# Two attention blocks on one core: a loop written out, head steps moved by one point, weights loaded in two halves

## What is computed

```python
# block 1: 32 query heads of 64 in 4 groups, window 128, per-head bias and sink
q, k, v, gate = split(rms(x) @ swa_w_in)
q, k = rms_norm(q, q_gain), rms_norm(k, k_gain)
p = exp(s - m); p = p / (sum(p) + exp(sink - m))
x = x + ((p @ v) * silu(gate)) @ swa_w_out
# block 2: 8 heads of differential attention (df) and 8 of stick-breaking attention (sb)
proj = rms(concat(meta, x)) @ w_in      # sb q,k,v,g and df q,k,v,g, each 1024 wide
dq = partial_rope(rms_norm_2(dq, q_norm_w)); dk = partial_rope(rms_norm_2(dk, k_norm_w))
df_o = (softmax(s0) - lam * softmax(s1)) @ dv        # then rms norm over 128
sb_o = exp(log_beta + tail) @ sb_v                   # tail: reversed cumulated log_keep
out = x + concat(sb_o * silu(sb_g), df_o * silu(df_g)) @ w_out
```

## Time and profile before

| | us |
|---|---|
| median of 3 runs (2010.58 to 2016.63) | 2014.16 |
| the profiled execution, its own time | 2015.65 |
| its span, first to last instruction | 2014.0 |
| PE busy | 1928.9 (96%) |
| PE weight loads busy | 1547.7 (77%) |
| DVE busy | 921.3 (46%) |
| ACT busy | 828.4 (41%) |
| POOL busy | 36.2 (2%) |

### The profile page before, as it was taken

The page is one execution under the profiler, slowest core; times in us unless marked ns, Lnnn a source line. Parts: engine busy times, 40 slices in busy tenths (PEclk is TensorE's granted clock), DMA queues, the critical chain, the costliest instruction groups (busy, mean ns, idle before and its releaser), DMA issues.

```text
span 2014.0 us, 28665 instructions
## 1 busy us (share of the span) xinstructions
PE 1928.9 (96%) x9868; PEld 1547.7 (77%) x9868; DVE 921.3 (46%) x2325; ACT 828.4 (41%) x1831; POOL 36.2 (2%) x65
## 2 busy tenths in 40 slices
PE   4999999898998999999999999999999999988999
PEld 3777777676776888878788887888878888766887
DVE  4355555555556333544445444454444445444222
ACT  5355455454555332534335343343433435244221
POOL 1000000000000000000000000000000000000000
PEclk9999999999998999999999999999999999989999
DMA  6932223122224445322222222222222322204553
GB/s 149 203 89 70 72 74 87 55 82 60 81 55 115 126 140 148 86 66 83 65 68 80 64 64 66 81 67 77 65 66 65 83 62 64 64 21 121 132 144 83
DMA packets 298414, 173.34 MB, mean 86 GB/s; under 512 B 23040, under 2 KB 289824, under 8 KB 297824
## 3 DMA queue, kind: packets, MB, share of 16 engines
q1 hardware_dynamic: 292976, 157.55, 29.1%
q0 software_dynamic: 4352, 13.98, 2.6%
q10 hardware_dynamic: 1024, 1.07, 0.3%
HBM read 156.86 MB, written 14.66 MB: 85 GB/s over the span
## 4 chain that ended last, share of the span: by engine, by line
PE 73%; ACT 9%; DVE 7%; issue 7%; DMA 3%; ACTq 1%; DVEq 0%; SPq 0%
PE G L448 58%; PE S L710 2%; ACT wh L853 2%; ACT p L940 2%; PE G L547 2%; DMA raw<-in_swa_w_in 1%; PE O L727 1%; PE S L755 1%; PE O L783 1%; ACTq L1113 1%; ACT pT L949 1%; ACT st L942 1%; PE T L701 1%; PE G L672 1%; DVE st L1352 1%
## 5 line engine op out<-in xcount | busy, mean ns | idle before, releaser
L448 PE MATMUL G<-xh,wh 128*128 128x512 f32 (+1 forms) x2624 | 898.0, 374 | 7.8 <-DVE xl L1424 4.8
L448 PE MATMUL G<-xl,wh 128*128 128x512 f32 (+1 forms) x2624 | 845.8, 354 | 0.0
L448 PE MATMUL G<-xh,wl 128*128 128x512 f32 (+1 forms) x2624 | 842.7, 353 | 0.0
L1270 DVE TENSOR_TENSOR wl<-raw,wh 128x512 fp32r<-128x512 f32 x528 | 353.8, 688 | 550.8 <-ACT wh L853 539.1
L448 PEld LDWEIGHTS G<-xh,wh 128*128 128x128 f32 x2624 | 465.8, 190 | 107.8 <-issue 36.0
L448 PEld LDWEIGHTS G<-xh,wl 128*128 128x128 f32 x2624 | 462.9, 189 | 70.1
L448 PEld LDWEIGHTS G<-xl,wh 128*128 128x128 f32 x2624 | 463.1, 189 | 66.0 <-issue 6.9
L853 ACT ACTIVATE wh<-raw 128x512 fp32r<-128x512 f32 x528 | 313.0, 619 | 190.8 <-DMA raw<-in_w_out 97.4
L1147 ACT ACTIVATE att<-att,st 128x144 f32<-128x144 f32 (+3 forms) x64 | 36.9, 576 | 187.9 <-DVE wmeta L1609 103.3
L940 ACT ACTIVATE p<-p,st 128x256 f32<-128x256 f32 (+1 forms) x128 | 60.8, 475 | 124.6 <-DVE st L1339 124.6
L1339 DVE CUSTOM_DVE_ANT_0 p<-S,bias,sink_u 128x256 f32<-128x256 f32 (+1 forms) x128 | 56.1, 442 | 0.0
(11 more groups left out here) (216 smaller groups left out, 1699.2 us busy)
## 6 DMA issues: line engine op xcount, KB each, us to landing
raw<-in_w_in SPq DMA_DIRECT2D x56, 1024.0 KB, 6.0
raw<-in_swa_w_in SPq DMA_DIRECT2D x32, 1024.0 KB, 5.5
raw<-in_swa_w_out SPq DMA_DIRECT2D x16, 1024.0 KB, 6.2
raw<-in_w_out SPq DMA_DIRECT2D x16, 1024.0 KB, 6.4
raw<-in_w_in POOLq DMA_DIRECT2D x8, 1024.0 KB, 7.4
rel_rows<-relb SPq DMA_DIRECT2D x1, 6128.0 KB, 36.7
mixed<-in_x SPq DMA_DIRECT2D x4, 1024.0 KB, 10.0
raw<-in_swa_w_in SPq DMA_DIRECT2D x8, 512.0 KB, 7.2
```

What stands on the lines that cost most here:

```text
L448: mm = pe.matmul(d, w[:, slot, k, :], v[:, k, a:b], start=(k == 0 and n == 0), stop=(k == KC - 1 and n == 2))
L1270: V.tensor_tensor(wl[:, slot, q, :], raw[:, slot, q, :], wh[:, slot, q, :].bitcast(F32), ALU.subtract).then_inc(w_lo, 1)
```

## The change

1. The loop over i = 1 to 3 of the first block is written out on all five engines. The instructions are the same ones in the same order, with constants in place of registers.
2. Each 1 MB weight load of SP becomes two of 512 KB. The first half is issued when DVE has split two quarters of the tile that held the slot, the second half when it has split all four. ACT waits for the first half before quarter 0 and for the second (`raw_late`) before quarter 2. The eight loads of sbq on POOL and those of the key and value tiles stay whole.
3. In `finish`, for dfq and dfk, the statistic on PE moves from point 1 to 2, the reciprocal root on ACT from 2 to 3, the scaling on DVE from 3 to 4, the four transfers on ACT from 4 to 5, and the three rotary passes on DVE from 6 to 7. OWNERS2 and its waits stay as they are.

```diff
-        gate_in, sbq_in = sem("gate_in"), sem("sbq_in")
+        raw_late = [sem(f"raw_late{i}") for i in range(2)]
+        sbq_in = sem("sbq_in")
@@ SP: weights()
-                after(sp, w_lo, 4 * (tile - 2) + 4)
-                sp.dma_start(raw[:, slot, :, :], w_v[:, :, ds(col, P)]).then_inc(raw_in[slot], 16)
+                for part, s in enumerate((raw_in[slot], raw_late[slot])):
+                    c = slice(part * KC // 2, part * KC // 2 + KC // 2)
+                    after(sp, w_lo, 4 * (tile - 2) + 2 * part + 2)
+                    sp.dma_start(raw[:, slot, c, :], w_v[:, c, ds(col, P)]).then_inc(s, 16)
@@ SP, POOL, PE, ACT, DVE alike
-            with sp.Fori(1, UNITS) as i:
+            for i in range(1, UNITS):
@@ ACT: split()
+                if quarter == 2 and loaded[0] is raw_in[slot] and len(loaded) == 2:
+                    act.wait_ge(raw_late[slot], loaded[1] - KV_LOADS)
@@ PE: finish()
-                    if p == 1:
+                    if p == 2:
                         norm_stat(two, 2 * h + ti + 1)
@@ ACT: finish()
-                    if p == 2:
+                    if p == 3:
                         after(act, n_stat, count)
...
-                    if p == 4:
+                    if p == 5:
                         buf, width = (dfk, ALL) if ti else (dfq, TOK)
@@ DVE: finish()
-                    if p == 3:
+                    if p == 4:
                         after(dve, n_rs, count)
...
-                    if p == 6:
+                    if p == 7:
                         after(dve, n_rot, 64 * count)
```

More of the change, by code:

```diff
@@ L310, in unit_loads @@
                 weights(T_UNIT + 2 * u, 0, w1_v, P * (4 * g + i))
-                after(sp, w_lo, 4 * (T_UNIT + 2 * u - 1) + 4)
-                sp.dma_start(raw[:, 1, :, :], w1_v[:, :, ds(SWA_GATE + P * (4 * g + i), P)]).then_inc(gate_in, 16)
+                weights(T_UNIT + 2 * u + 1, 1, w1_v, SWA_GATE + P * (4 * g + i))
             for g in range(KV):
                 unit_loads(0, g)
-            with sp.Fori(1, UNITS) as i:
+            for i in range(1, UNITS):
                 for g in range(KV):
@@ L418, in _ @@
                 sinks_of(0, g)
-            with pool.Fori(1, UNITS) as i:
+            for i in range(1, UNITS):
                 for g in range(KV):
@@ L581, in _ @@
                 swa_window(0, g, attend=g > 0)
-            with pe.Fori(1, UNITS) as i:
+            for i in range(1, UNITS):
                 for g in range(KV):
@@ L825, in _ @@
             KV_LOADS = 2 * 16 * (KV // 2)
-            OUT1_LOADS = (KV_LOADS + 16 * 4 * UNITS, KV_LOADS)
+            OUT1_LOADS = (KV_LOADS + 16 * 4 * UNITS, KV_LOADS + 16 * 4 * UNITS)
             HEAD_LOADS = tuple(n + 16 * (KC // 2) for n in OUT1_LOADS)
@@ L830, in kv_loaded @@
             def kv_loaded(g):
-                return (raw_in[g % 2], 32 * (g // 2 + 1)) if g < KV else unit_loaded(0, 0)
+                return (raw_in[g % 2], 32 * (g // 2 + 1), "whole") if g < KV else unit_loaded(0, 0)
             def unit_loaded(u, half):
-                return (gate_in, 16 * (u + 1)) if half else (raw_in[0], KV_LOADS + 16 * (u + 1))
+                return raw_in[half], KV_LOADS + 16 * (u + 1)
             def out_loaded(loads, i, slot):
@@ L846, in split @@
             def split(pair, slot, quarter, loaded):
+                if quarter == 2 and loaded[0] is raw_in[slot] and len(loaded) == 2:
+                    act.wait_ge(raw_late[slot], loaded[1] - KV_LOADS)
                 if quarter == 0:
-                    act.wait_ge(*loaded)
+                    act.wait_ge(*loaded[0:2])
                     after(act, tile_done, 2 * pair + slot - 1)
@@ L998, in _ @@
                 swa_window(0, g, attend=g > 0)
-            with act.Fori(1, UNITS) as i:
+            for i in range(1, UNITS):
                 for g in range(KV):
@@ L1414, in _ @@
                 swa_window(0, g, attend=g > 0)
-            with dve.Fori(1, UNITS) as i:
+            for i in range(1, UNITS):
                 for g in range(KV):
```

## The result

The changed kernel takes 2029.14 us (median of 5 runs, 2025.29 to 2032.61) against 2014.16 us before. The ratio is 1.0075 with a 95% interval of 1.0055 to 1.0096, so it is slower by 15 us. The forecast was 2019.1 us with a range of 2009 to 2029: the sign was right, the loss three times too small, and the time lies just outside the range. What came out is nearly rival B's 2030 us. Of the experiments' runs one is left out of its figure: an execution of e1_unroll that took 2820 us at a mean granted clock of 0.626.

A forecast was written before the change was run, and what follows sets the result against it. PE's own instruction stream was taken to bound heads 1 to 7, with under 0.2 us margin at tile boundaries. -11.6 - 1.5 + 17.5 + 0.5 = +4.9 us on 2014.16 gave 2019.1 us, range 2009 to 2029.

The forecast's parts named there:

- rival B: Heads: new stops also slow PE's clock, each head losing 1.5 us more; +10.7 us in sum, 2030 us; chance 0.08.
- Part 1: First block: writing out the loop saves 11.6 us, covering both jumps back and register costs per unit.
- Part 2: First query tile: the first half load lands sooner, cutting PE's wait for the squares; -1.5 us.
- Part 3: Heads: later statistic and rotary steps make PE wait; +17.5 us over seven heads, +0.5 in head 0.
- A head costs 2.4 - 1.0 + 1.0 = 2.4 to 2.5 us: Each of heads 1 to 7: dfq wait, less the returned statistic stop, plus dfk wait.
- The wait for dfq: Start of tile dfv: PE waits 2.4 us for dfq's last rotary pass, ending at 1209.05 against 1206.64 wanted.
- The walk through the three engines: One head, followed through PE, ACT and DVE: 12.7 us from dfq's statistic to its last rotary pass.
- The wait for dfk: Start of tile dfg: PE waits 1.0 us more for dfk's last rotary pass.
- The credit for the statistic's stop: Dfk's statistic finds its squares ready; the 0.83 us stop and queue refilling return about 1.0 us a head.
- The granted clock: Heads: clock loss behind new stops, left out of the forecast sum; as a rival 1.5 us a head, chance 0.08.
- A: Heads: PE doesn't wait at the banks and the statistic's stop goes; -20.1 us, 1994 us; chance 0.17.
- C: First block: writing out brings nothing, instruction stalls come at intervals of code; +6.4, 2020.6 us with half loads; chance 0.05.

The follow-up runs named there:

- e1_unroll: Kernel before with only the first block's loop written out on all five engines: 2002.20 us, ratio 0.9940.
- e6: Kernel before with the first block's loop written out on VectorE (DVE) alone, loops kept on the other four engines: 2007.04 us, ratio 0.9959.
- e11: Kernel before, loop kept, with the query tile's weight load in units 4 to 15 issued one quarter of VectorE's splits later: 2010.44 us, ratio 0.9969.
- e2: Kernel before with only the weight loads in two halves, loop and steps as before: 2008.93 us, ratio 0.9975.
- e8: Changed kernel with only the three rotary passes put back to point 6; statistic, root, scaling and transfers stay one point later: 2004.27 us, ratio 0.9951.
- e3: Kernel before with only the statistic and rotary steps one point later: 2046.04 us, ratio 1.0149.
- e10: Kernel before with only the banks of dfq and dfk released by n_ln, the statistic's last reader: 2013.45 us, ratio 0.9990.
- e7: Changed kernel with statistic, root, scaling and transfers at their old points, only the three rotary passes one point later: 2027.11 us, ratio 1.0060.
- e5: Changed kernel with dfv, dfg and sbq waiting for n_ln (last reader of the banks) instead of the last rotary pass: 1985.97 us, ratio 0.9857.

## Why the prediction was right or wrong

**Part 1, the loop written out: right.** Forecast -11.6. The units took 10.9 us less between the first two points shown (32.1 us each), and e1 alone is 12 us faster. What the forecast took from the Trainium skill (Runtime: NRT & Kernel Launch, Instruction fetch mechanics), that a taken branch out of the two pages in memory must fetch before it goes on, is borne out by e6, where the two stops go with VectorE's loop, and by the row of instructions in e11. The stop was 5.1 us with 1 MB of weights under way, 3.3 with 0.5 MB, and 2.6 with none. That half loads would also shorten it I had missed. It made no difference to the sum, since the change removes the jumps themselves.

**Part 2, the half loads: right in size.** Forecast -1.5 at the first query tile. The changed kernel is 1.96 us ahead there, and TensorE's wait for the squares fell from 2.76 to 0.49 us. It was forecast at about 1.2. The half was there 1.2 us behind the end of the write of `rel_rows` (91.08 and 89.89), and not 1.4. In e2, with the same loads, that write ended 1.3 us later than before, the wait is 1.38 us and the kernel 0.8 us ahead, so the size differs from one profile to the next.

**Part 3, the steps: the mechanism right, the sum too small by half.** The step that failed is the sum of a head, "A head costs 2.4 - 1.0 + 1.0 = 2.4 to 2.5 us". Measured is 26.4 / 7 = 3.8 us. Its terms:

- *The wait for dfq*, forecast 2.4, measured 2.61. The walk through the three engines was 0.2 us off over 12.9 us.
- *The wait for dfk*, forecast 1.0, measured 1.41. Here the walk leant on "no key activations" and wider passes by round sums. e8 has 1.0 us for dfk without the late passes, so part of this wait comes from the other four later steps, which I had under-sized.
- *The credit for the statistic's stop*, forecast -1.0, measured -0.83. These three terms make 3.2 us instead of 2.5, 4.9 us over seven heads.
- *The granted clock*, put at nothing in the sum, measured 5.1 us of lost clock over seven heads, or 4.5 us of time. In this profile it falls at each of the seven stops for dfq, and less often at the small products that follow.

The clock was rival B, with a chance of 0.08. Its price per head (1.5 us) was that of one fall. That its 2030 us lies so near the measured time is in part luck: it had 2.5 us of waits and 1.5 of clock a head, and measured are 3.2 and about 0.6. I had set it aside on one row, a clock of 1.00 behind a 2.76 us stop. One row did not carry that. In the profile of e1_unroll the same stop, 2.54 us long, does have a fall behind it:

```profile
101.00:105.00 4.00, 4.00 (x10) 2.44 (x11) 1.99 (x4) 2.15 (x4) 0.00 (x0) 0.57 0.44 126
```

e6 has it there too (stop 2.77 us), as have e3 (2.4) and e11 (1.9), and the kernel before (2.76) and e10 (2.77) have not. So whether a stop of the same length there is followed by a fall differs from one profile to the next. At the seven stops of 2.6 us in the heads it came each time, in the changed kernel and in e3, but only twice in seven in e7: 16 of 21 in all. I had the other term of B wrong as well: in the kernel before a fall came in six of seven heads at the small products. A new fall took the place of some of these, and only three were added in sum. The written-out loop took two away, one behind each jump: the stretches 350 to 365 and 480 to 510 us have a mean clock of 0.89 and 0.94 before and 1.00 after. Over the whole span the lost clock is 29.2 us before and 30.2 after.

**Rivals A and C** fell. PE did wait at the banks, and the written-out units are 32.1 us apart with no new idle. C's sum was wrong as well: without the 11.6 us the other terms give -1.5 + 17.5 + 0.5 = +16.5, that is 2030.7 us, and its +6.4 and 2020.6 follow from none of them.

**Left open:** what decides whether a fall comes at a stop or at the small products (there two times in seven heads after the change, three to six in the kernels without the stops, seven in e7), and VectorE's second stop of 1.5 us behind a jump. A second 8 KB of instructions lands 1.4 us before that stop ends (at 356.03 in the kernel before), but no run varied it.

## What to carry to other kernels

When a step is moved to a later point, list who waits for its semaphore, with the margin that the trace shows there. Here two margins of 0.2 us stood behind a semaphore that promised more than the waiter needed; waiting for the last reader of the bank instead turned a loss of 15 us into a gain of 28 (e5). And when a new stop of a few us appears on a TensorE that was always busy, price the half clock behind it as the likely case (16 of 21 stops of 2.5 to 2.6 us here), not as a rare one, and count which falls elsewhere it takes the place of.

## What the runs showed of the hardware that I had not expected

- VectorE's stop at a jump back depended on what else was being transferred: 5.1 and 4.8 us with a 1 MB load under way, 3.2 and 3.3 us with 0.5 MB, 2.6 and 2.3 us with none (1.9 of it is usual there without a jump).
- Each fall of the granted clock in the heads had the same size, in every kernel here: 3.4 us at the lower level, 1.7 us of clock lost, 1.5 us of time. At the end of the last head, where TensorE stops for 4.6 us, longer stretches of 6.8, 10.2 and 13.7 us are seen too.
- A long stretch without a stop does not keep the clock up: e5's TensorE never waits in the heads, and the clock still fell at the small products in three heads of seven.
